# Expert loop of a hybrid decoder step: the high half of the gate weights is formed on ScalarE behind the SiLU, not on VectorE

## The reference

```python
def expert_block(args):
    xblk, e = args
    return (jax.nn.silu(xblk @ w_gate[e]) * (xblk @ w_up[e])) @ w_down[e]
yb = lax.map(expert_block, (xb, blk_e)).reshape(rows, -1).astype(F32) * row_w[:, None]
```

## Time and profile before

| | |
|---|---|
| median of 3 runs | 4498.65 us (4485.08 to 4503.09) |
| the profiled execution | 4505.88 us, its span 4504.4 us |
| busy share of the span | PE 80%, DVE 48%, ACT 30%, POOL 13% |
| expert loop in that execution | from 3392.0 to 4394.5 us, 48 blocks, 32 experts |

### The profile page before, as it was taken

How to read it: one execution, slowest core, us unless ns; L and a number is a source line. 1 busy time by engine, 2 the same in 40 slices (tenths; PEclk the granted TensorE clock), 3 DMA queues, 4 the chain that set the end, 5 groups by cost and what they waited for, 6 DMA issues and landing times. The chain is left out here.

```text
span 4504.4 us, 56440 instructions
## 1 busy us (share of the span) xinstructions
PE 3593.8 (80%) x18387; PEld 2865.9 (64%) x18441; DVE 2162.5 (48%) x2864; ACT 1370.8 (30%) x2532; POOL 579.6 (13%) x296
## 2 busy tenths in 40 slices
PE   6888789888886888882587799678847989989990
PEld 5777668677775777772343677357745777777770
DVE  4665533233333566663221566223337766685643
ACT  4433321133334233332121232224412333333320
POOL 0000000000000000002120000101103444343412
PEclk9898889987788999996687899778868999999995
DMA  5555555522233011112352333222327777786748
GB/s 210 194 188 188 189 221 227 198 84 75 78 100 107 31 35 35 35 35 83 103 164 97 110 127 113 95 84 95 96 84 276 255 264 263 261 292 243 258 194 312
DMA packets 322314, 686.94 MB, mean 153 GB/s; under 512 B 82699, under 2 KB 118716, under 8 KB 316063
## 3 DMA queue, kind: packets, MB, share of 16 engines
q1 hardware_dynamic: 266118, 503.21, 33.1%
q0 software_dynamic: 37552, 142.36, 8.9%
q10 hardware_dynamic: 18576, 40.51, 2.3%
HBM read 527.09 MB, written 193.16 MB: 160 GB/s over the span
## 5 line engine op out<-in xcount | busy, mean ns | idle before, releaser
L136 PE MATMUL inu_po<-inu_w,inu_nT 128*128 128x512 f32 (+1 forms) x680 | 260.3, 383 | 82.7 <-DVE inu_nT L131 67.6
L2613 POOL TENSOR_TENSOR ex_down<-ex_down_raw,ex_down 128x2048 fp32r<-128x2048 f32 x32 | 199.2, 6225 | 495.4 <-ACT ex_down L2689 495.4
L137 PE MATMUL inu_po<-inu_w,inu_nT 128*128 128x512 f32 (+1 forms) x680 | 253.2, 372 | 0.0
L138 PE MATMUL inu_po<-inu_w,inu_nT 128*128 128x512 f32 (+1 forms) x680 | 252.6, 371 | 0.0
L739 PE MATMUL att_outp<-att_va,att_pT 128*128 128x65 f32 x1200 | 210.0, 331 | 52.6 <-DVE att_pT L681 52.5
L739 PEld LDWEIGHTS att_outp<-att_va,att_pT 128*128 128x128 f32 x1200 | 196.4, 246 | 69.4 <-DVE att_pT L681 48.6
L674 DVE TENSOR_REDUCE att_res<-att_score 128x4 f32<-128x1024 f32 (+1 forms) x96 | 90.8, 986 | 264.6 <-PE att_score L710 162.3
L136 PE MATMUL ex_py<-ex_down,ex_hT 128*128 128x512 f32 x384 | 161.1, 420 | 68.3 <-POOL ex_down L2613 40.2
L136 PEld LDWEIGHTS inu_po<-inu_w,inu_nT 128*128 128x128 f32 x680 | 137.9, 203 | 111.2 <-DVE inu_nT L131 64.3
L2716 ACT ACTIVATE ex_late<-ex_py 128x512 f32<-128x512 f32 x96 | 52.2, 596 | 510.0 <-PE ex_py L138 510.0
L136 PE MATMUL inq_po<-inq_w,inq_nT 128*128 128x512 f32 x408 | 165.1, 405 | 32.8 <-DVE inq_w L526 32.8
(11 more groups left out here) (566 smaller groups left out, 9043.4 us busy)
## 6 DMA issues: line engine op xcount, KB each, us to landing
ex_gate_raw<-in_w_gate SPq DMA_DIRECT2D x32, 2048.0 KB, 12.0
ex_up_raw<-in_w_up SPq DMA_DIRECT2D x32, 2048.0 KB, 11.1
ex_down_raw<-in_w_down POOLq DMA_DIRECT2D x32, 2048.0 KB, 9.0
inu_big<-tmp_u SPq DMA_DIRECT2D x192, 192.0 KB, 3.1
tmp_yb<-ex_late ACTq DMA_DIRECT2D x48, 512.0 KB, 7.2
tmp_nT<-inu_nT SPq DMA_DIRECT2D x17, 1024.0 KB, 5.2
inq_nT<-tmp_nT SPq DMA_DIRECT2D x17, 1024.0 KB, 5.1
out_win_k<-in_cache_k SPq DMA_DIRECT2D x8, 2032.0 KB
```

What stands on the lines that cost most here:

```text
L136: pe.matmul(out, ah, bh, start=start, stop=False)
L137: pe.matmul(out, ah, bl, start=False, stop=False)
L138: return pe.matmul(out, al, bh, start=False, stop=stop)
L2613: return eng.tensor_tensor(half["d"][:, 1, k], raw["d"][:, k], half["d"][:, 0, k].bitcast(F32), ALU.subtract)
```

## The change

ScalarE gets a third conditional piece, right behind the SiLU of block b: if b+1 is the first block of its expert, it writes the high half of that expert's gate weights (`upper("g")`). VectorE's piece for the gate weights keeps its place ahead of `hh`, but no longer writes the high half and no longer waits for the DMA; it waits for ScalarE's high half and writes the low half. The head of the loop (expert 0) is as it was: there ScalarE made the high half already.

```diff
@@ ScalarE, work(i, u, b)
                     act.activation(sg, gu[:, 0, :], ACT.Silu).then_inc(E["sg_ok"], 1)
+                    with act.If(first(act, b + 1)):
+                        upper("g", expert(act, b + 1) + 1)
                     with act.If(first(act, b)):
                         r = expert(act, b) + 1
@@ VectorE
-                def halves(p, r):
-                    dve.wait_ge(E[p + "_in"], 16 * r)
-                    split(dve, half[p][:, 0], half[p][:, 1], raw[p][:], E[p + "_hi"], r).then_inc(E[p + "_split"], 1)
-
                 def lower(p, r):
                     dve.wait_ge(E[p + "_hi"], r)
                     dve.tensor_tensor(half[p][:, 1], raw[p][:], half[p][:, 0].bitcast(F32), ALU.subtract).then_inc(E[p + "_split"], 1)
@@ VectorE, work(i, u, b)
                     with dve.If(first(dve, b + 1)):
                         dve.wait_ge(E["gate_mm"], b + 1)
-                        halves("g", expert(dve, b + 1) + 1)
+                        lower("g", expert(dve, b + 1) + 1)
```

## The result

The changed kernel takes 4720.18 us (median of 6 runs, 4706.16 to 4733.69), the kernel before 4499.75 (6 runs, 4485.08 to 4503.37): ratio 1.0498 [1.0471, 1.0524], slower. The profiled execution took 4718.09 us, span 4716.6. The range and the chance of slower held, and the mechanism too: 214 us were forecast and 220.4 lie between the medians. One term, that of the blocks with D alone, was off by 11.5 us.

What follows compares the result with a forecast made beforehand. TensorE was taken to bound the expert loop. Terms of 116 (G alone), 113 (the blocks with both), 3 (block 0) and -18 (D alone) sum to 214 us on the profiled 4505.9: 4720, as median 4713; range 4660 to 4775.

Steps and rivals of the forecast that it cites:

- D alone: 15 blocks that are an expert's first with no new expert next: 20.7 us each, 310 against 328, -18 us.
- The place of the high half: Behind the SiLU, ScalarE's high gate half starts 3.8 us after the y copy; `hh` at 11.8 instead of 5.5.
- G alone: 14 blocks before a new expert, not themselves a first block: 26.7 us against 18.43, 116 us in all.
- The price in clock: TensorE's work after the gap before `hh`: lower clock adds 2.0 us to each block with G alone.
- The rival in which the clock stays down longer: TensorE after the gap: gate product runs at 1.2 GHz to its end; time 4796 us, chance 0.15.
- The blocks with both: 16 blocks that are an expert's first and precede a new expert: 28.3 us against 21.24, 113 us in all.
- VectorE's takes 4.5 to 5.3 there: Sign in the blocks with both: VectorE's half of the down weights takes 4.5 to 5.3 us.
- The loss of clock is covered: The blocks with both: gate product, slowed by 2.0 us, ends at 21.0, before the down product at 22.5.
- The rival without lock: At the down weights GpSimd and VectorE share, or VectorE comes first: 26.7 us per block, time 4687, chance 0.17.
- 0.2 for clock: Clock allowance in us within the 20.7 forecast for each block with D alone.
- the start of the high down half: On ScalarE in blocks with D alone: a skipped branch's read delays it by 0.4 us (0.4 to 0.9).
- The faster rival: High half ready before `hh` needs it; six blocks waiting for `ex_hT` give back 35 us: 4464, chance 0.03.

Runs made afterwards that it cites:

- Kernel 1: Against the kernel before: ScalarE makes the high gate half one block earlier in its queue, ahead of the y copy; 4498.74 us, ratio 1.0022.
- kernel 8: Against the changed kernel: ScalarE makes the high gate half behind the high down half instead of ahead of it; 4767.88 us, ratio 1.0599.
- Kernels 3 and 5: 3: changed kernel plus 22 extra TensorE matmuls before the `hh` wait ahead of a new expert, 1.0551; 5: also GpSimd's low down half after VectorE's, 1.0370.
- kernel 4: Against the changed kernel: GpSimd starts its half of the low down weights only when VectorE's is done; 4695.84 us, ratio 1.0447.
- kernels 2 and 9: Both start GpSimd's low down half only after VectorE's: 2 against Kernel 1, ratio 0.9951 (repeat 0.9976); 9 against the kernel before, ratio 0.9958.

## Why the prediction was right, step by step

**The place of the high half: right.** ScalarE's piece was forecast 3.8 behind the y copy; it starts at 3.8 on average, in 22 of the 30 blocks between 3.5 and 4.0 (3.1 to 5.2 in all). `hh` was forecast at 11.8, measured 12.0 on average in G alone and 11.6 with both; the wait at 6.3 each and some 190 in total, measured 6.3 on average and 188.7 in the 30 blocks (200.2 with block 0). Kernel 1 shows that place, and not the work, is the cause; kernel 8 shows it from the other side.

**The price in clock: right, a little too high.** In G alone `hh` to y copy takes 14.64 on average, 1.7 above 12.9 where I took 2.0. That `hh` came 0.2 later than forecast made up for it, and so 26.67 stands against 26.7. Kernels 3 and 5 confirm that this part is clock: with the gap filled, 12.9 returns at PEclk 1.00. The rival in which the clock stays down longer (4796) fell.

**The blocks with both: right, but the cover is thinner than I said.** GpSimd's half ends at 16.0 (forecast 16.3), VectorE's at 18.2 (18.5), the down product starts at 22.2 (22.5), the y copy comes at 28.0 (28.3). VectorE's half starts 0.6 behind `hh`, not 1.5: it waited for GpSimd inside its instruction instead of ahead of it. So the sign "VectorE's takes 4.5 to 5.3 there" was wrong (6.05 to 6.08), while the end is the same. "The loss of clock is covered" holds in 13 of 16; in blocks 10, 16 and 30 the clock fell a second time, behind the 1.9 to 2.15 us wait for `ex_hT`, and they took 29.9 to 30.4. The Trainium skill (SBUF — State Buffer, Who interferes with whom) says that a VectorE instruction with two SBUF inputs contends with a GpSimd instruction that reads SBUF. The traces agree: the two halves take 2.28 and 4.57 in kernel 4, where they stand one behind the other, and 6.07 and 5.30 in the change, where they meet. The rival without lock priced these blocks at 26.7, and kernel 4, which orders the two, gives 26.46: its price was good, its condition didn't hold.

**D alone: the term that was mis-sized.** Forecast 15 x 20.7 and -18; measured 21.46 and -6.5, so 11.5 us too little cost. The order came as said: VectorE is first in all 15, and none of them waits for `ex_hT`. But of the five slow blocks only block 23 became normal (20.52); blocks 3, 11, 41 and 43 still take 22.2 to 22.9. Two terms were too small. The larger is "0.2 for clock": in six of the 15 (3, 11, 13, 35, 41 and 45) the clock fell behind the wait of 2.0 to 2.8 us for GpSimd, at 1.6 each, which is 0.65 a block and 6.8 us over the sum. Blocks 33 and 35 show it, TensorE's first matmul of the down product in each:
```profile
4264.26 0.49 PE L136 MATMUL ex_py<-ex_down,ex_hT 128*128 128x512 f32 x1 [2.03 <-POOL ex_down L2613]
...
4311.26 0.79 PE L136 MATMUL ex_py<-ex_down,ex_hT 128*128 128x512 f32 x1 [2.05 <-POOL ex_down L2613]
```
The same wait to 0.02 us, full clock in the one and half in the other: 20.53 and 22.14 for the block. I had the row of a normal block and took it for all.

The other term is the start of the high down half, which accounts for the remaining 4.7 us. ScalarE's idle time ahead of it was taken 0.4 longer; in the usual block it is 0.57 longer (block 33: 1.97 instead of 1.40), and in blocks 3, 11, 17, 31, 41 and 43 it is 2.1 to 3.7. Blocks 33 and 43:
```profile
4253.74 3.63 ACT L2689 ACTIVATE ex_down<-ex_down_raw 128x4096 fp32r<-128x4096 f32 x1 [1.97 <-issue]
...
4503.89 3.62 ACT L2689 ACTIVATE ex_down<-ex_down_raw 128x4096 fp32r<-128x4096 f32 x1 [3.65 <-issue]
```
Neither wait ends with a DMA or another engine in the profile, so what lies in it is not shown beyond the register reads and branches that stand there.

**The other side.** The faster rival named its condition (the high half done before `hh` needs it) and its gain (35 us from the six blocks that wait for `ex_hT`). Kernel 1 meets the condition, and the gain did not come: the six waits stayed, at 29.0 us. What frees those blocks is the order at the down weights alone (kernels 2 and 9).

**What went into the forecast of the time.** 4713 against 4720: the loop lost 12 more than forecast, 11.5 of it in D alone and 2.4 in the blocks with both (the second falls), less 2 in G alone and block 0. That the profiled execution (4718) met the 4720 forecast for it is luck: the head of the program was 13 us shorter in it. The upper end of the range doesn't follow from its reasons: half way into the clock case is 4755, and the dearer read makes it 4762, not 4775. The measured time lies inside either.

## What to carry to other kernels

Before a piece of work goes to the idler engine, look at where that engine's idle time stands in its in-order queue, not at how much it has: 72.5 us of work that nobody waited for cost 220 us behind the SiLU and nothing measurable ahead of the y copy. Check next which engine then comes first at a resource that the two share; here one semaphore wait that sets this order gained some 0.4%, and the moved cast nothing. And price a gap on TensorE at more than its length, since the work behind it may run at half clock.

## What the runs showed of the hardware

- Gaps of nearly one length end in either clock. Of the gaps of 2.00 to 2.25 us ahead of the down product in the blocks of D alone, in all twelve traces, 24 of 45 were followed by matmuls at half clock; of those under 1.75 us none of 56, and of those over 3 us 15 of 16. What decides between them is open.
- Filling one gap can move the fall of the clock into the next: kernel 3 kept TensorE at full clock through most gaps before `hh` and lost 1.2 us per block with both at the wait behind it. More work for TensorE (1103.83 us busy instead of 965.34) at a higher clock (0.94 instead of 0.90) made a longer loop (1250.9 instead of 1228.2).
- The length of an instruction's record contains its wait for the other engine: GpSimd's half of the down weights shows 4.5 to 4.6 us when VectorE is in none of its subtractions and 5.28 to 5.31 when it starts inside VectorE's gate subtraction (changed kernel), and VectorE's gate subtraction 5.36 instead of 4.43 beside GpSimd in kernel 8's block 7.
